# Three quarters of the output product moved into the stage ahead of the inverse, with the head norms and the first weight loads in another order

## The reference

```
proj  = rms_norm(x, norm_mix) @ w_in
o_A   = gated_delta(conv+silu(q,k,v), beta, g)     # 8 heads x 64, chunks of 64 tokens
        # t_inv = inverse(I + low), low = strict lower part of (beta k k^T) * decay
        # u = t_inv (beta v), w = t_inv (beta k e^G); per chunk: v_new = u - w S,
        # o = q_head S + qk v_new, S = S e^g + k_tail^T v_new
o_A   = rms_norm(o_A per head, gdn_norm) * silu(z)
o_B   = stick_breaking(q, k, v)                    # 8 heads x 64, paged cache for decode
x     = x + concat(o_A, o_B) @ w_out               # the output product
x     = x + moe(rms_norm(x, norm_ffn))             # top 4 of 32 experts, 1024 -> 2048 -> 1024
y     = rms_norm(x, norm_final)
```

## Time and profile before

| | us |
|---|---|
| median of 3 runs | 1277.05 |
| lowest, highest | 1274.8, 1283.34 |
| the profiled execution | 1282.89 |
| its span in the profile | 1281.2 |
| PE busy | 1217.6 (95% of the span) |
| DVE, ACT, POOL busy | 422.6, 237.5, 87.6 |
| DMA | 464.75 MB, 363 GB/s over the span |

### The profile page before, as it was taken

One profiled execution on the slowest core, in us unless ns is written; L12 is line 12 of the kernel. 1 busy time (PEld: TensorE's weight loads), 2 busy tenths in 40 slices (PEclk: granted clock), 3 DMA queues, 4 the chain that ended last, 5 costly groups with the idle time before them and its releaser, 6 DMA issues.

```text
span 1281.2 us, 18705 instructions
## 1 busy us (share of the span) xinstructions
PE 1217.6 (95%) x7378; PEld 528.3 (41%) x7378; DVE 422.6 (33%) x887; ACT 237.5 (19%) x417; POOL 87.6 (7%) x162
## 2 busy tenths in 40 slices
PE   8999898899999999999999999999999999999996
PEld 6756566684533333333333333333333333333332
DVE  3568726435522222232222222132232222221323
ACT  2312247222201101110110111010111101110103
POOL 6103203422000000000000000000000000000000
PEclk9999999999999999999999999999999999999999
DMA  9999971205889999999999999999999999999994
GB/s 269 261 302 345 328 263 35 89 8 208 314 354 430 425 427 429 427 427 430 429 425 428 429 429 426 429 429 427 427 429 428 425 431 428 427 427 428 428 428 183
DMA packets 71305, 464.75 MB, mean 363 GB/s; under 512 B 16959, under 2 KB 17087, under 8 KB 44631
## 3 DMA queue, kind: packets, MB, share of 16 engines
q1 hardware_dynamic: 71208, 463.89, 90.5%
q10 hardware_dynamic: 46, 0.18, 0.1%
HBM read 460.33 MB, written 3.70 MB: 362 GB/s over the span
## 4 chain that ended last, share of the span: by engine, by line
PE 56%; DMA 23%; issue 1%; ACT 1%; DVE 0%; SPq 0%; DVEq 0%; ACTq 0%
PE bank L2146 26%; DMA ring<-in_w_up 21%; PE bank L2179 7%; PE bank L2115 4%; PE bank L2094 4%; PE bank L2159 3%; PE bank L1603 2%; DMA ring<-in_w_down 2%; PE bank L2098 1%; PE bank L2119 1%; PE bank L1458 1%; PE bank L1468 1%; PE bank L1465 1%; PE bank L2206 1%; PE bank L2135 0%
## 5 line engine op out<-in xcount | busy, mean ns | idle before, releaser
L2146 PE MATMUL bank<-ring,work 128*64 128x512 f32 x1280 | 286.9, 601 | 19.2 <-DMA ring<-in_w_up 19.2
L2179 PE MATMUL bank<-ring,work 128*64 128x512 f32 x768 | 172.5, 596 | 9.0 <-ACT work L2281 5.8
L2146 PEld LDWEIGHTS bank<-ring,work 128*64 128x64 f32 x1280 | 89.2, 138 | 214.2 <-issue 186.2
L509 PE MATMUL bank<-hoT,ring 128*128 128x288 f32 x448 | 115.5, 414 | 3.3 <-DMA ring<-in_w_in 2.8
L2380 DVE TENSOR_SCALAR work<-bank 128x512 f32<-128x512 f32 x32 | 22.0, 688 | 231.5 <-PE bank L2159 230.5
L2179 PEld LDWEIGHTS bank<-ring,work 128*64 128x64 f32 x768 | 55.2, 137 | 104.6 <-issue 103.3
L509 PEld LDWEIGHTS bank<-hoT,ring 128*128 128x128 f32 x448 | 84.7, 193 | 29.7 <-issue 4.2
L2265 ACT ACTIVATE work<-bank 128x1024 f32<-128x1024 f32 x16 | 16.4, 1023 | 384.4 <-PE bank L2098 363.6
L2339 DVE TENSOR_TENSOR Xw<-Xw,bank 128x512 f32<-128x512 f32 x64 | 44.0, 687 | 121.0 <-PE bank L2115 121.0
L2393 DVE COPY work<-bank 128x512 f32<-128x512 f32 x16 | 11.1, 691 | 212.8 <-PE bank L2179 212.8
L2115 PE MATMUL bank<-work 128*128 128x512 f32 x128 | 59.2, 605 | 0.0
(11 more groups left out here) (415 smaller groups left out, 1300.8 us busy)
## 6 DMA issues: line engine op xcount, KB each, us to landing
ring<-in_w_up SPq DMA_DIRECT2D x96, 2048.0 KB, 24.9
ring<-in_w_down SPq DMA_DIRECT2D x48, 2048.0 KB, 26.9
work<-in_w_up SPq DMA_DIRECT2D x16, 2048.0 KB, 25.1
hoT<-in_w_up SPq DMA_DIRECT2D x16, 2048.0 KB, 29.5
ring<-in_cache_k SPq DMA_DIRECT2D x64, 256.0 KB, 10.4
ring<-in_cache_v SPq DMA_DIRECT2D x64, 256.0 KB, 10.2
work<-in_w_down SPq DMA_DIRECT2D x16, 1024.0 KB, 22.7
hoT<-in_w_down SPq DMA_DIRECT2D x16, 1024.0 KB, 24.6
```

The costliest lines, as they stand in the source:

```text
L509: ins = pe.matmul(bank[0:m, i % 2, 0:T], w[:, k, :], hT[:, k, :], start=k == 0, stop=k == KD - 1)
L2146: ins = pe.matmul(bank[CAP * e:CAP * e + CAP, g, :], xT[:, k, CAP * e:CAP * e + CAP], weight(odd, ch + e, k % 2 * RSLOT + 512 * g), start= ...
L2179: ins = pe.matmul(bank[CAP * e:CAP * e + CAP, 4 + m, :], aT[:, k, CAP * e:CAP * e + CAP], weight(odd, ch + e, k % 4 * D + 512 * m), start= ...
```

## The change

In stage 2 the calls of `keep_busy` go, and `project_part` makes three of the four quarters `first` in their places, in banks 1, 3 and 4, as soon as each head pair's output is copied and the bank is free. In stage 3 DVE adds these three banks to `X` first of all. PE waits for the first addition ahead of group B's first turn and for all three ahead of the first level's second half. The later `project(0, 0)`, `project(0, 1)` and `project(1, 0)` then cover `second` alone. The squares' sum of B moves ahead of the decode output; the decode tokens' first halves come before the sum of D, their second halves after the first `normed`. `rstd` and `normed` go in the order D, A, B, and PE waits for one, two and three of them in turn. In SP's queue chunk 0 is issued after the squares' sums, chunk 6 after the decode values are spread, chunk 1 after the last `normed`, and the six bias loads behind these. Some banks change their number.

```diff
+        s_wo, s_wor = sem("mixer_out"), sem("residual_added")
+        PART_BANK = {(0, 1): 1, (0, 0): 3, (1, 0): 4}
+        PARTS = len(PART_BANK)
...
-                def keep_busy(n):
-                    for _ in range(n):
-                        pe.matmul(bank[:, 1, :], ident[:], work[:, 0:512], start=True, stop=True)
+                def project_part(t, m, ps):
+                    w = slot(U_WO + 2 * m, 2).rearrange("p (k n) -> p k n", k=KD)
+                    for p in ps:
+                        ins = pe.matmul(bank[:, PART_BANK[t, m], :], oT[:, HP + p, toks(t)], w[:, HP + p, :],
+                                        start=p == 0, stop=p == HP - 1)
+                    return ins
...
                 values(2)
                 turn_kv(3)
                 products(2)
-                keep_busy(3)
+                slot_wait(pe, U_WO)
+                slot_wait(pe, U_WO + 2)
+                pe.wait_ge(s_beta, DECODE_ROUNDS + 3)
+                pe.wait_ge(s_poe, 2)
+                project_part(0, 1, (0, 1))
+                pe.wait_ge(s_beta, DECODE_ROUNDS + 4)
+                project_part(0, 0, (0, 1))
                 turn(3)
                 turn_kv(4)
                 values(3)
                 products(3)
-                keep_busy(1)
+                pe.wait_ge(s_poe, 3)
+                project_part(0, 0, (2,))
                 products(4)
-                keep_busy(4)
+                project_part(0, 1, (2,))
+                pe.wait_ge(s_poe, 4)
+                project_part(0, 1, (3,)).then_inc(s_wo, 1)
+                project_part(0, 0, (3,)).then_inc(s_wo, 1)
+                pe.wait_ge(s_ATe, DECODE_ROUNDS + 4)
+                project_part(1, 0, range(HP)).then_inc(s_wo, 1)
...
-        WO_BANK = {(2, 0): 4, (2, 1): 6, (0, 0): 3, (0, 1): 5, (1, 0): 7, (1, 1): 1}
-        TURN_BANK = {2: slice(6, 7), 0: slice(3, 5), 1: slice(6, 8)}
+        WO_BANK = {(2, 0): 5, (2, 1): 7, (0, 0): 3, (0, 1): 4, (1, 0): 6, (1, 1): 1}
+        TURN_BANK = {2: slice(7, 8), 0: slice(3, 5), 1: slice(6, 8)}
...
+                sp.wait_ge(d_ss, 3)
+                load_chunk(sp, 0, 0)
+                sp.wait_ge(d_pool, SCALED["v_by_sequence"])
+                load_chunk(sp, 0, 6)
                 sp.wait_ge(d_nrm, 3)
+                load_chunk(sp, 0, 1)
                 for g in range(4):
                     sp.dma_start(bu[NE * g:NE * g + NE, :], b_up[0, :, 512 * g:512 * (g + 1)]).then_inc(s_bias, 16)
                 for m in range(2):
                     sp.dma_start(bd[NE * m:NE * m + NE, :], b_down[0, :, 512 * m:512 * (m + 1)]).then_inc(s_bias, 16)
-                sp.wait_ge(d_pool, SCALED["v_by_sequence"])
-                for ch in (0, 1, 6):
-                    load_chunk(sp, 0, ch)
                 sp.wait_ge(s_ringfree, U_END - U_WO)
                 for ch in (4, 5):
                     load_chunk(sp, 0, ch)
...
                 def turn_T(g):
                     pe.wait_ge(d_T[g], 1)
+                    if g == "B":
+                        pe.wait_ge(s_wor, 1)
...
                 def level_p(g, l):
                     pe.wait_ge(d_Ye[g], l)
                     pe.wait_ge(d_T[g], l)
+                    if l == 1:
+                        pe.wait_ge(s_wor, PARTS)
...
-                                        start=k >= HP if t == 2 else k == HP, stop=k < HP if t == 2 else k == HP - 1)
+                                        start=k >= HP if t == 2 else k == (HP if (t, m) == (1, 1) else 0),
+                                        stop=k < HP if t == 2 else k == HP - 1)
...
                 first, second = range(HP, KD), range(HP)
-                slot_wait(pe, U_WO)
-                slot_wait(pe, U_WO + 2)
-                project(0, 0, first)
+                norm_sums("B", 2, bank[:, 3, :])
                 pe.wait_ge(d_vn, 5)
                 for p in range(HP):
                     for a in range(2):
                         ins = pe.matmul(bank[pr(a), 0, ND * p:ND * p + ND], ub(vn, 16 + p, a), ub(QK, 16 + p, a, col=LO),
                                         start=True, stop=True)
                 ins.then_inc(d_o, 1)
-                project(0, 1, first)
+                pe.wait_ge(d_St, 4)
+                for m in range(2):
+                    project(2, m, first)
                 pe.wait_ge(d_ot, 1)
-                norm_sums("B", 2, bank[:, 2, :])
                 norm_sums("D", 3, bank[:, 0, P:2 * P])
-                pe.wait_ge(d_St, 4)
-                project(1, 0, first)
                 pe.wait_ge(d_ln, 1)
                 project(1, 1, first)
-                pe.wait_ge(d_nrm, 3)
+                pe.wait_ge(d_nrm, 1)
                 for m in range(2):
-                    project(2, m, (*first, *second)).then_inc(s_wo, 1)
+                    project(2, m, second).then_inc(s_wo, 1)
+                pe.wait_ge(d_nrm, 2)
+                pe.wait_ge(d_ln, 2)
                 project(0, 0, second).then_inc(s_wo, 1)
                 project(0, 1, second).then_inc(s_wo, 1)
+                pe.wait_ge(d_nrm, 3)
                 pe.wait_ge(d_pool, SCALED["v_by_sequence"])
                 state_update(0)
...
                 pe.wait_ge(s_rw, 128)
                 logits(0, 2)
-                pe.wait_ge(s_wo, 6)
+                pe.wait_ge(s_wo, PARTS + 6)
                 pe.sem_inc(s_ringfree, U_END - U_WO)
...
-                    act.wait_ge(d_ln, n)
+                    act.wait_ge(d_ln, 3)
...
-                log_sums(2, bank[:, 2, :], 512)
+                log_sums(2, bank[:, 3, :], 512)
                 log_sums(3, bank[:, 0, P:2 * P], P)
+                rstd(3, P)
                 rstd(1, 512)
                 rstd(2, 512)
-                rstd(3, P)
...
-                    act.wait_ge(s_wor, i + 1)
+                    act.wait_ge(s_wor, PARTS + i + 1)
...
+                for t in range(2):
+                    dve.wait_ge(s_x[t], 32)
+                for i, ((t, m), b) in enumerate(PART_BANK.items()):
+                    dve.wait_ge(s_wo, i + 1)
+                    x = X[:, t, 512 * m:512 * (m + 1)]
+                    dve.tensor_tensor(x, x, bank[:, b, :], ALU.add).then_inc(s_wor, 1)
...
-                def normed(n, o, w, gate, dst):
-                    dve.wait_ge(d_rs, n)
+                def normed(i, n, o, w, gate, dst):
+                    dve.wait_ge(d_rs, i + 1)
...
-                normed(1, bank[:, O_BANK["A"], :], 512, zg[:, :, 0:P], oT[:, 0:HP, 0:P])
-                normed(2, bank[:, O_BANK["B"], :], 512, zg[:, :, P:SEQ], oT[:, 0:HP, P:SEQ])
                 dve.wait_ge(d_ot, 1)
-                normed(3, otm[:, 1024:1152], P, zg[:, :, SEQ:T], oT[:, 0:HP, SEQ:T])
+                normed(0, 3, otm[:, 1024:1152], P, zg[:, :, SEQ:T], oT[:, 0:HP, SEQ:T])
+                normed(1, 1, bank[:, O_BANK["A"], :], 512, zg[:, :, 0:P], oT[:, 0:HP, 0:P])
+                normed(2, 2, bank[:, O_BANK["B"], :], 512, zg[:, :, P:SEQ], oT[:, 0:HP, P:SEQ])
 
                 def residual(t, i):
                     dve.wait_ge(s_x[t], 32)
+                    dve.wait_ge(s_wor, PARTS)
...
-                            dve.wait_ge(s_wo, m + 1)
+                            dve.wait_ge(s_wo, PARTS + m + 1)
...
-                            dve.wait_ge(s_wo, 3 + 2 * t + m)
+                            dve.wait_ge(s_wo, PARTS + 3 + 2 * t + m)
```

More of the change, by code:

```diff
@@ L1378, in build @@
         assert 10660 + P <= CONST_END
-        s_wo, s_wor = sem("mixer_out"), sem("residual_added")
         lg, mk, ex, gtr, eq, ce = (at(3340 + 96 * i, (3, NE)) for i in range(6))
```

## The result

The changed kernel takes **1270.52 us** (median of eight runs, 1265.65 to 1272.33). The kernel before takes 1279.55 beside it (eight runs, 1274.8 to 1283.34). The ratio is 0.993, with a 95% interval of 0.9915 to 0.9946, so 6.9 to 10.9 us are gained, 9.0 by the medians. Compared again on two chips the ratio was 0.9921 [0.9897, 0.9946] and 0.9924 [0.9895, 0.9953]. The profiled execution of after takes 1269.83, its span is 1268.1.

A forecast was written before the change was run, and what follows sets the result against it. PE's work ahead of the expert loop sets its start, to which the end is tied, though the DMA stream bounds the loop later. -10.9 + 0.8 = -10.1 us gave 1267.0 us, range 1262 to 1273 with rivals.

The forecast's parts named there:

- the forecast by itself: The whole kernel without any rival coming in: 1267.0 us, 1264 to 1270 with the spread of runs, chance 0.58.
- rival 2: Ahead of the loop, part of the gain becomes a wait for norms, decode rows or code: 1269 to 1272, chance 0.20.
- The bound: Expert loop to end: the DMA stream bounds it late, but the end is tied to the loop's start.
- Rival 3: The stream does not follow, so time given back ahead of the loop is lost: 1277 to 1278 us, chance 0.06.
- The removed products: Stage 3's output product: three quarters leave, 24 instructions, 10.9 us less.
- The handover to stage 3: End of stage 2: PE, with the added products, ends the stage at 235.4 instead of 234.66, plus 0.8 us.
- The norms: Output product in stage 3: in the new order PE waits for none of the norms, margins about 1 us each.
- if PE stood behind the norms: Stage 3: one of the signs that would show the prediction wrong.
- Additions and loads: Inverse stage: three DVE additions, 2.1 us, hidden by idle time; earlier chunk loads gain nothing for themselves.
- Clock and code: Inverse stage: the half clock for some 4 us and late code beside the earlier loads were both counted as nothing.
- rival 1: Early inverse stage: the clock stays at its upper level, 2.1 us more gain, 1264.9 us, chance 0.13.
- this trace disagrees: PE's 2.21 us stand at 243.8 in the inverse stage, taken as late code, against code crossings being mostly hidden.

The follow-up runs named there:

- fillers: Changed kernel with eight filler instructions (3.70 us of PE) put ahead of the third state update, just behind the first logits: 1274.34 us, ratio 0.9977.
- pool_waits: Changed kernel with GpSimd's scaling of the old decode states held until the third normed group is done: 1269.34 us, ratio 0.9939.
- old_loads: Changed kernel with the loads of chunks 0, 1 and 6 back behind the bias loads, at their old time: 1268.82 us, ratio 0.9936.
- parts_only: Kernel before with only the three quarters moved to stage 2; norms, narrow products and loads keep the old order: 1275.26 us, ratio 0.9969.
- order_only: Changed kernel with the fillers back in stage 2 and all 96 product instructions in stage 3, new order kept: 1279.65 us, ratio 0.9991.
- after_again: The changed kernel measured once more, unedited: 1271.29 us beside 1279.2 for the kernel before.
- after_third: The changed kernel measured once more, unedited, on another chip: 1270.81 us beside 1279.47 for the kernel before, ratio 0.9924.
- all_late: Changed kernel with norm weights, chunk 3 and router weights loaded at the end of the inverse stage, not its start: 1269.49 us, ratio 0.9934.
- late_ordered: Changed kernel with all four loads late, the small ones ahead of chunk 3, and the biases ahead of chunk 0: 1264.99 us, ratio 0.989.
- best: late_ordered with the edit of pool_waits added: 1266.2 us, ratio 0.9895.
- late_chunk3: Changed kernel with only the load of chunk 3 moved from the start of the inverse stage to its end: 1266.98 us, ratio 0.9892.

## Why the prediction was right, and where its sizes were off

**The number.** 1267.0 was forecast, 1270.52 measured, within the range of 1262 to 1273, and within 1% of before, as the likeliest case had it. It is 0.5 above the 1264 to 1270 of the forecast by itself and lies where rival 2 had the time. Of the 3.5 us between them 2.5 is the base: eight runs of before have a median of 1279.55 where three had 1277.05. By differences it is 10.1 forecast and 9.0 measured, with 6.9 to 10.9 possible. Two sizes below are off by about 0.3 us in opposite directions, which is luck.

**The bound.** Right. In every profile the loop to the end takes 936.9 to 937.2 us, whatever the loop's start, and fillers shows it by time as well: 3.7 us put back ahead of the loop cost 5. Rival 3 is refuted.

**The removed products.** Right in kind, a little too large: 24 instructions of 0.453, 10.9 us. From start to start of the single instructions in the trace, the 48 full ones of before take 21.20 us and the 24 that are left 10.66, so 10.5 went. The fourth column fell by 9.11, and the rest of the difference is the stand of the norms and the small products, two and three points down.

**The handover to stage 3.** The sign was right, 0.8 was too much: 0.52. PE's last product ends at 232.85 and VectorE's chain at 231.20 + 1.41 = 232.61, so PE does end the stage as forecast. Counted from the stage's start the turn of head pair 3 came 0.30 later and the last seven products started 0.24 later, where 0.4 was forecast for both; these products took 6.28 and not 6.35; and the forecast's 235.4 against 234.66 had been rounded up from 0.73 to 0.8.

**The norms: the failed step.** "It waits for none of them; the margins are about 1 us each." PE waited 1.00 us for the decode rows. The logarithms and exponentials came in the order that I worked out, and some 0.7 late: the exponentials at 288.23, where the forecast's 291.4, less the 3.85 by which this stretch began earlier, is 287.6. PE was late by as much (next point), so that was no loss. But I had priced VectorE's first multiply at 0.28 from the row of before, where GpSimd was idle. These are the rows of VectorE and GpSimd in before:

```profile
300.77 0.28 DVE L1892 TENSOR_TENSOR ring<-ring 128x128 f32<-128x128 f32 x1
```

```profile
290.58 3.68 POOL L1842 TENSOR_TENSOR ring<-ring,work 128x2048 f32<-128x2048 f32 x1
295.35 0.19 POOL L1847 MEMSET gq<- 128x102 f32 x1
```

In its new place it stands beside GpSimd's scaling and takes 1.92. A margin of 0.9 can't hold 1.6 more. pool_waits shows this: with that one instruction elsewhere the multiply takes 0.29, and PE's wait is gone. I had looked at the queues that the moved steps pass, and not at what runs on GpSimd meanwhile, though the profile of before had the instruction at 290.58 to 294.26. The prediction named "if PE stood behind the norms" as a sign of being wrong, and on this point it was. The margin behind it held: VectorE had the decode rows normed at 304.27 and PE's transposes of them start at 305.36, 1.1 us later, where some 1.5 were forecast.
The page "SBUF — State Buffer" of the Trainium skill (section "SBUF: two separate sides") has GpSimd and VectorE share one pair of ports, under an exclusive lock, for a VectorE instruction with two SBUF inputs against a GpSimd one that reads SBUF. By that rule, the trace agrees: the multiply with two SBUF inputs was held to GpSimd's end, and the addition with one input in PSUM at 284.61, beside GpSimd's other instruction, took its usual 0.29. This rule spoke against the change, and I did not use it. This is rival 2's case (1269 to 1272) in its first form, at half of its smallest price.

**Small products, not counted.** From start to start, the narrow products are now two groups of 16 of 1.85 us each, 3.71 instead of 3.57 (the prediction had 1.6 for a group); and the sum of the decode squares stands alone in front of the quarter, so that the sums take 1.38 instead of 1.08. Together some 0.4 us. So 10.54 less 1.00 less 0.44 is 9.10, against 9.11 read.

**Additions and loads.** Right. VectorE's three additions took 1.88 us at 233.27 and nobody waited for them; old_loads shows no worth of the new loads.

**Clock and code.** Right for the three profiles of the changed kernel: the clock falls behind the stand in the inverse stage, though the gap at the end of stage 2 is closed. The window 244 to 245 of after has 0.50, as 247 to 248 had the earlier trace rows:

```profile
244.00:245.00 1.00, 1.00 (x24) 1.00 (x22) 0.75 (x2) 0.00 (x0) 0.00 (x0) 0.50 0.00 0
```

But it does not fall there every time. parts_only, old_loads, fillers and pool_waits have the same work up to there, the same early loads and the gap closed; they stand 1.35 to 1.63 us, and the clock stays at its upper level behind it. This is fillers, PE's timeline and a window:

```profile
242.01 0.38 PE L1488 MATMUL bank<-ring 64*64 64x64 f32 x5 [1.63 <-issue]
```

```profile
242.00:244.00 2.00, 1.99 (x68) 1.99 (x70) 1.27 (x2) 0.00 (x0) 0.00 (x0) 1.00 0.10 29
```

In before and order_only, with the gap, it fell both times, behind 2.21. So rival 1 did not come in the change's own profiles, but it is not out for every execution, and whether the closed gap has a part in it stays open. Its price of 2.1 was too high: the third column has about 1.1 for one stretch at the lower level. The loads at 286.5 cost no stand in PE's long instructions.
The page "TensorE: Matmul & The Clock Gate" of the Trainium skill (section "Why this matters for your kernels") has gaps bring the clock down. By that rule, the trace agrees in part: the clock fell behind stands of 1.90 to 4.32 us in this stage, but in after_again, after_third, parts_only and old_loads it also fell at 264 to 273, behind nothing longer than 0.41.

What I had not seen is that the stand and the low clock can be removed for free: they go when the loads leave the stage, which is worth half of the change (4.3 to 5.8 by the medians). That the stand is code arriving late is argued from its place and from its going with the loads; no run here shows the fetch itself. The prediction's "this trace disagrees" rests on the same argument.

## What to carry to other kernels

When work is taken off the path, ask what it covered: here the new order of the norms gave nothing that shows by itself and half of the gain together with the move. When a step is moved, look at what the other engines run at its new time, for an instruction's duration is that of its neighbours too. And when a stretch has a stand that the profile gives no cause for, beside a transfer that nobody needs soon, move the transfer first: moving the one line of chunk 3 was worth 4.3 us, moving four load lines 5.8 with the small loads ahead of the large ones, and nearly nothing without.

## What was not expected of the hardware

- PE stands 1.35 to 4.32 us in streams of 64x64 products while loads are running or have just landed, and at most 0.48 when none are (all_late, late_ordered, best). The page "Runtime: NRT & Kernel Launch" of the Trainium skill (section "Instruction fetch mechanics") has the crossing of a code block mostly hidden; if that is what these stands are, the runs disagree.
- Near such idle times the granted clock fell to 0.50 in after (1.90 us), after_third (2.17), before and order_only (2.21), all_late (2.55), parts_only (3.59) and after_again (4.32). It stayed at 1.00 behind 1.35 us in old_loads, 1.63 in parts_only, fillers and pool_waits, 1.85 in late_chunk3, and behind the 1.00 us in after.
- The clock also falls with PE busy throughout, at 323 to 325 in after and 336 to 338 before, in the router. It is absent in parts_only, pool_waits and fillers, and those that have it take some 1.7 us longer for that stretch (20.7 against 19.0, without the 3.5 that the fillers take); in order_only it lasts from 331 to 337 and the stretch takes 22.5. What decides it stays open. The windows of after:

```profile
323.00:324.00 1.00, 1.00 (x2) 0.48 (x2) 0.90 (x6) 0.00 (x0) 0.00 (x0) 0.50 1.12 475
324.00:325.00 1.00, 1.00 (x2) 0.34 (x2) 0.04 (x1) 0.00 (x0) 0.00 (x0) 0.50 0.82 328
```
